# Folded products for the mixers' output gates and branch gates

## What is computed

```python
h = rmsnorm_2(x, mix_norm[l])
hq, hf, hi, hg, aq, ak, av, ga, gb = jnp.split(h @ w_in[l], split_idx, axis=-1)
...
o_a = hgrn2_chunk_scan(q_a, k_a, v_a, log_f)
o_a = rms(o_a.reshape(b, t, HG_HEADS, HG_DV)).reshape(b, t, HG_WV)
o_a = o_a * hgrn_out_norm[l].astype(f32) * jax.nn.silu(hg.astype(f32))
y_a = o_a.astype(x.dtype) @ w_branch_a[l]
...
y_b = o_b.astype(x.dtype) @ w_branch_b[l]        # o_b: dilated window attention, 4 heads of 3 groups
merged = jax.nn.sigmoid(ga) * y_a + jax.nn.sigmoid(gb) * y_b
x = x + merged @ w_out[l]
```

## Time and profile before

| | |
|---|---|
| median of 3 runs | 3286.3 us (3283.62 to 3288.35) |
| the profiled execution's own time | 3285.39 us |
| its span in the profile | 3283.6 us |
| mean granted TensorE clock | 0.998 of full speed |
| PE busy | 3246.1 us, 99% |
| DVE busy | 2387.8 us, 73% |
| ACT busy | 1341.4 us, 41% |

### The profile page before, as it was taken

One profiled execution on the slowest core, in us unless ns is written; L12 is line 12 of the kernel. 1 busy time (PEld: TensorE's weight loads), 2 busy tenths in 40 slices (PEclk: granted clock), 3 DMA queues, 4 the chain that ended last, 5 costly groups with the idle time before them and its releaser, 6 DMA issues.

```text
span 3283.6 us, 49474 instructions
## 1 busy us (share of the span) xinstructions
PE 3246.1 (99%) x18769; PEld 2836.5 (86%) x18769; DVE 2387.8 (73%) x3047; ACT 1341.4 (41%) x1809; POOL 611.4 (19%) x514
## 2 busy tenths in 40 slices
PE   8999999999999999999999999999999999999999
PEld 4888888888888888888888899999888889999988
DVE  4877857868787635556778877866888886875887
ACT  3222233212232224333536455356645445446643
POOL 2212322202321130002223220000223230000122
PEclk9999999999999999999999999999999999999999
DMA  6645514645265433334665664435666665443664
GB/s 227 204 153 172 160 46 135 201 140 186 89 199 172 135 99 94 90 103 145 198 177 167 195 182 146 123 117 146 184 191 178 195 183 161 122 122 110 195 196 147
DMA packets 863528, 507.66 MB, mean 155 GB/s; under 512 B 15093, under 2 KB 843569, under 8 KB 863345
## 3 DMA queue, kind: packets, MB, share of 16 engines
q1 hardware_dynamic: 862976, 503.74, 51.5%
q0 software_dynamic: 368, 1.38, 0.1%
HBM read 504.01 MB, written 1.05 MB: 154 GB/s over the span
## 4 chain that ended last, share of the span: by engine, by line
PE 92%; DVE 4%; ACT 2%; issue 1%; SPq 0%; DMA 0%; DVEq 0%; ACTq 0%
PE bank L661 18%; PE bank L663 18%; PE bank L662 18%; PE bank L659 17%; PE bank L657 10%; PE bank L656 2%; PE bank L1112 2%; DVE wlo_all L1508 1%; PE bank L776 1%; PE bank L966 1%; ACT whi_all L1179 1%; DVE t_full L1682 1%; PE bank L1005 1%; PE bank L1010 0%; PE bank L907 0%
## 5 line engine op out<-in xcount | busy, mean ns | idle before, releaser
L1508 DVE TENSOR_TENSOR wlo_all<-raw,whi_all 128x1024 fp32r<-128x1024 f32 (+3 forms) x768 | 1007.0, 1313 | 493.2 <-ACT whi_all L1179 490.7
L1179 ACT CAST whi_all<-raw 128x1024 fp32r<-128x1024 f32 (+3 forms) x768 | 834.4, 1090 | 896.6 <-PE bank L663 563.8
L661 PE MATMUL bank<-xn_two,whi_all 128*128 128x512 f32 (+1 forms) x2592 | 894.0, 345 | 2.9 <-DVE xn_two L1674 2.6
L663 PE MATMUL bank<-xn_two,wlo_all 128*128 128x512 f32 (+1 forms) x2592 | 872.5, 337 | 0.0
L662 PE MATMUL bank<-xn_two,whi_all 128*128 128x512 f32 (+1 forms) x2592 | 872.5, 337 | 0.0
L659 PE MATMUL bank<-xn_two,whi_all 128*128 128x512 f32 x1540 | 549.3, 396 | 0.0
L661 PEld LDWEIGHTS bank<-xn_two,whi_all 128*128 128x128 f32 x2592 | 491.4, 190 | 55.3 <-issue 4.3
L662 PEld LDWEIGHTS bank<-xn_two,whi_all 128*128 128x128 f32 x2592 | 491.5, 190 | 51.0 <-issue 0.7
L663 PEld LDWEIGHTS bank<-xn_two,wlo_all 128*128 128x128 f32 x2592 | 490.9, 189 | 51.5
L657 PE MATMUL bank<-xn_two,wlo_all 128*128 128x256 f32 x1760 | 455.7, 279 | 1.0 <-DVE xn_two L1674 0.9
L2148 POOL CAST h_two<-silu_g 128x256 f32 (+1 forms) x176 | 202.7, 1152 | 1339.8 <-DVE silu_g L1740 771.6
(11 more groups left out here) (323 smaller groups left out, 4280.1 us busy)
## 6 DMA issues: line engine op xcount, KB each, us to landing
raw<-in_ffn_w_in SPq DMA_DIRECT2D x176, 512.0 KB, 3.7
raw<-in_w_in SPq DMA_DIRECT2D x168, 512.0 KB, 3.7
ada_w<-in_ada_w SPq DMA_DIRECT2D x128, 512.0 KB, 3.7
raw<-in_ffn_w_gate SPq DMA_DIRECT2D x88, 512.0 KB, 3.7
raw<-in_ffn_w_up SPq DMA_DIRECT2D x88, 512.0 KB, 3.8
raw<-in_ffn_w_down SPq DMA_DIRECT2D x32, 768.0 KB, 5.1
raw<-in_ret_w_in SPq DMA_DIRECT2D x48, 512.0 KB, 3.9
raw<-in_ffn_w_out SPq DMA_DIRECT2D x32, 768.0 KB, 5.2
```

The lines of the kernel that those rows point to most:

```text
L661: pe.matmul(o, whi[s][:, k, :], hi, start=(k == 0), stop=False)
L663: return pe.matmul(o, wlo[s][:, k, :], hi, start=False, stop=(k == ks - 1))
L1179: act.copy(whi[s][:, 0:ks, :], raw[s][:, 0:ks, :]).then_inc(hi_done[s], 1)
L1508: tt(wlo[s][:, 0:ks, :], raw[s][:, 0:ks, :], whi[s][:, 0:ks, :].bitcast(F32), ALU.subtract).then_inc(lo_done[s], 1)
```

## The change

The units of `hg` and `gates` use folded products. DVE adds the bank's halves with one `tensor_reduce` into the gate's own tile and frees the bank; ACT does `split_hi` first, waits for that sum, and applies Silu or Sigmoid in place. A counter `gf` tells DVE how many gates are done. Besides, the semaphore `onehot_ready` is gone, and PE's first `sum` of a mixer waits for `zero`, which POOL raises a little later in its own order.

```diff
                 gained, ready = normed(a["norm"])
                 moving = pair(xn2_two, SEQ)
+                beside = pair(xn2_two, SEQ, True)
...
-                    source = dict(br_b=attended, hf=gained).get(ph, moving)
+                    source = dict(br_b=attended, hf=gained, hg=beside, gates=beside).get(ph, moving)
...
                     if c == 0:
-                        pe.wait_ge(onehot_ready, 1)
+                        pe.wait_ge(hg["zero"], l + 1)
...
-                def take(dst, func):
-                    def evacuate(s, k, r):
-                        act.activation(dst[:, k, :], bank[s][:, 0:SEQ], func).then_inc(bank_free[s], 1)
-                    return evacuate
+                def take_output_gate(s, k, r):
+                    act.wait_ge(bank_free[s], r + 2)
+                    act.activation(g_g[:, k, :], g_g[:, k, :], ACT.Silu).then_inc(hg["gf"], 1)
...
                 def take_gates(s, k, r):
                     dst = gates_a[:, k, :] if k < DC else gates_b[:, k - DC, :]
-                    act.activation(dst, bank[s][:, 0:SEQ], ACT.Sigmoid).then_inc(bank_free[s], 1)
+                    act.wait_ge(bank_free[s], r + 2)
+                    act.activation(dst, dst, ACT.Sigmoid).then_inc(hg["gf"], 1)
...
-                    if ph in ("hq", "hf"):
+                    if ph in ("hq", "hf", "hg", "gates"):
                         split_hi(s, r + 1, p["ks"] if it + 1 < p["rounds"] else next_ks[p["name"]])
                         takes[ph](s, SLOTS * it + s, r)
                         return
...
+                def gated(n):
+
+                    dve.wait_ge(hg["gf"], 3 * HH * l + n)
...
+                    if ph in ("hg", "gates"):
+                        dst = g_g[:, k, :] if ph == "hg" else gates_a[:, k, :] if k < DC else gates_b[:, k - DC, :]
+                        dve.tensor_reduce(dst, bank[s][:].rearrange("p (c t) -> p t c", c=2), AXX,
+                                          ALU.add).then_inc(bank_free[s], 1)
                     if ph == "br_b":
-                        after_act("gates", 2 + it, s)
+                        gated(2 * HH + k + 1)
...
                     if j == 0:
-                        for s in range(SLOTS):
-                            after_act("hg", 1, s)
+                        gated(HH)
...
                     link(pool.memset(onehot, 0.0))
                     link.after()
-                    pool.memset(onehot[:, P - 1:P], 1.0).then_inc(onehot_ready, 1)
+                    link(pool.memset(onehot[:, P - 1:P], 1.0))
+                    link.after()
```

More of the change, by code:

```diff
@@ L470, in build @@
         hg = {k: sem(f"hg_{k}") for k in ("d", "mm", "cp", "x", "xe", "o", "oe", "sq", "ss", "rt", "rr", "sp",
-                                          "hm", "of", "ohi", "olo", "mf", "mhi", "mlo", "zero", "qf")}
-        onehot_ready = sem("onehot_ready")
+                                          "hm", "of", "ohi", "olo", "mf", "mhi", "mlo", "zero", "qf", "gf")}
         lb_d = sem("lb_d")
@@ L1392, in do_mixer @@
                 takes = dict(att_qk=take_qk, hi=take_values(0), att_v=take_values(2), hq=take_query,
-                             hf=take_forget, hg=take(g_g, ACT.Silu), gates=take_gates)
+                             hf=take_forget, hg=take_output_gate, gates=take_gates)
                 def apply(k):
```

## The result

The changed kernel takes 3291.82 us (median of 20 runs, 3289.54 to 3294.07); the kernel before, run beside it, takes 3286.01 us (median of 20, 3283.51 to 3288.91). The ratio is 1.0017 with a 95% interval of 1.0011 to 1.0023: 5.8 us slower, clearly not nothing, and a little under the 6.6 us that the prediction set as its own bound for "slower".

A forecast was written before the change was run, and what follows sets the result against it. PE's own work plus its waits was taken to bound the kernel. Per mixer, 5.2 us more waiting less 1.7 gained gives 3.5, both 7.0: 3285.4 becomes 3292.4, or 3293 on the runs' median; range 3286 to 3299.

The forecast's parts named there:

- the walk: Likeliest case (chance 0.52): following the engines' lists, six points per mixer where PE waits come later; 3292.4 us.
- PE's gain: Folded units on PE save 0.07 us each: 1.7 us a mixer, 3.4 us in all.
- Step 1: hsum: split_hi and an open table load at unit 60 delay ACT's copies 1.4 us; PE waits 0.3 us.
- Step 2: hspread(3): unit 63's sum and gate precede round 0's exponentials; PE's shift 0.74 us, 0.9 more waiting.
- Step 3: turn_probs of round 1: ACT from unit 68 to scale takes 8.9 us, was 7.31; PE waits 1.8 us more.
- Steps 4 and 6: attend, rounds 1 and 2: ACT waits for DVE's sums of units 71 and 76; PE waits 0.8 and 1.1 more.
- Step 5: turn_probs of round 2: no load laid open, only order; shift 3.0 us, PE waits 0.4 us more.
- The end of the mixer: After attend of round 2, seven units at -0.07 us follow; the mixer ends 3.5 us later.
- Costs taken at nothing: PE's wait on zero, DVE's gated waits and PE's waits for a bank were each charged 0 us.
- Half of it: Rival (chance 0.28): a load stays hidden or sums slip into gaps; 1.3 to 2 us a mixer less, 3289.
- DVE falls behind: Rival (chance 0.07): late split_lo makes PE wait for weights, 4.9 us a mixer, 3302 us.
- A switch that stands open costs twice as much: Rival (chance 0.05): each newly opened table load holds ACT 2.7 us, not 1.29; 3298 us.

The follow-up runs named there:

- experiment 8: Experiment 6 with plain products and DVE's copy in place of the sum of halves, so without folding: 3278.69 us, ratio 0.9977.
- experiment 6: Changed kernel with ACT's in-place gate functions put off and run as one group a round, behind side work: 3276.05 us, ratio 0.9967.
- experiment 3: Changed kernel plus a one-column function ahead of ACT's wait for units 60 and 68, loading the tables early: 3289.14 us, ratio 1.0011.
- experiment 9: Changed kernel with only unit 63's gate function moved behind round 0's exponentials: 3290.25 us, ratio 1.0012.
- experiment 10: Kernel before, with only split_hi put ahead of the function in hg and gates; no folding, no DVE work: 3288.42 us, ratio 1.0007.
- experiment 7: Experiment 3 with only the gate functions of units 71 and 76 put behind their unit's side work: 3284.75 us, ratio 0.9996.

## Why the prediction was right, and where it was off

The forecast was 3293 us (7.0 us slower); it is 3291.8 (5.8 slower, 6.1 in the stretch). The likeliest case, the walk, is what happened. Its mechanism was shown step by step, not only its sum.

*PE's gain.* Taken as 0.07 us a unit, it is 0.075 (experiment 8): 0.08 in a row of units, as the earlier trace rows against the earlier trace rows had given, and about 0.06 for one that begins behind side work (2.90 us against 2.96 for unit 67 in experiments 6 and 8). So this term was right, and it explains nothing of the difference between 7.0 and 6.1. That lies in steps 2 to 6: each was 0.1 to 0.2 us too large, 0.7 us in a mixer, and at the end of the mixer 0.2 us less came back than I had said, which by luck made the sum look better than its steps.

*Step 1, hsum:* +0.28 for +0.2, and gone when the load is hidden (experiment 3).

*Step 2, hspread(3):* +0.54 for +0.74. Unit 63's gate is the cause of the rise there (experiment 9 takes +0.54 to -0.05). Experiment 3 brings this point to +0.06 with that gate in its place, but by another way: PE comes there 0.4 us earlier because hsum does, and the rise from hspread(2) to hspread(3) stays (+0.43, for +0.50 in the changed kernel and -0.11 in experiment 9). The exponentials' load came as late as forecast: 2192.03 against 2190.31, less the 0.87 us of the profile's own lateness, is 0.85 for 0.84. But from that load to the last split_hi ahead of hspread(3) it is 6.83 us (2198.86, shown in experiment 9) against 7.07 in the earlier trace rows: the gate of unit 65, now behind this split_hi, gave back 0.24 where I had counted 0.10.

*Step 3, turn_probs of round 1:* +1.34 over step 2 for the +1.5 of the walk. The chain took 8.81 us for 8.9, and unit 68 ended 0.4 us late for 0.6. A load laid open, shown twice: taken away from the changed kernel, 1.39 us (experiment 3), and added to the kernel before, +1.41 (experiment 10).

*Steps 4 and 6, the attends:* +0.58 and +0.89 for +0.7 and +1.0, from two gates queued ahead of the copies and waiting for DVE (experiment 7 takes both away). ACT in round 2, in answer to the earlier trace rows:

```profile
2248.72 0.42 ACT L1381 ACTIVATE gates_b<-gates_b 128x256 f32<-128x256 f32 x1 [0.71 <-DVE gates_b L1897]
2249.04 1.22 ACT L1442 COPY a_pt<-bank 128x512 f32<-128x512 f32 x3
```

Scale began at 2243.86, so it is 5.18 us to the copies: 5.3 in the walk, 4.28 before.

*Step 5, turn_probs of round 2:* the step that was wrong in kind, if only by a tenth. I charged order +0.1; it is -0.04. From the exponentials to scale it is 4.20 us after and 4.16 before: no load is laid open and the gate that moved behind split_hi costs nothing there.

*The end of the mixer:* it returned 0.27 us where I had said 0.5. I had counted seven changed units behind attend of round 2, and there are six (78 to 83), 0.45 us; why the rest didn't come back was not looked into. Two more slips changed nothing: the added waits of the walk sum to 5.3 us and not 5.2, and four of its six points, not three, are places where the earlier trace rows show a wait.

*Costs taken at nothing.* They were nothing: in both mixers PE has no new wait for a bank, for wlo_all or for `zero`. The sum of halves took 0.69 us as in the earlier trace rows.

*The rivals.* "Half of it" was wrong: no load slipped back by itself, it takes an instruction to pull it (experiment 3). "Folding gives nothing" fell with experiment 8. "DVE falls behind" had no sign in the waits. "A switch that stands open costs twice as much" asked for some 2.7 us at a load laid open, and experiment 10 has 1.41; of the drain that the Trainium skill gives in "ScalarE: Activation LUTs", What ACT_TABLE_LOAD costs, neither this run nor any other here shows anything. Had it held, the stretch would have been near +11.6.

*What I overlooked.* The prediction finds no wait of today that is shortened. For the change as it was made that is right. But the change also takes the bank's release away from ACT, and with it the reason for running the functions at once. That is worth 16 us between the changed kernel and experiment 6 (17 in the stretch), more than anything in the forecast.

## What to carry to other kernels

Fold products where the engine that multiplies does not wait; elsewhere a part of the saving (0.08 us in 2.88) is paid out in waiting, and the moved work decides. When a bank's emptying moves to another engine, the function that follows has lost its hurry: take it out of the strict list, and run several under one table load in time in which ACT waits anyway. And walk the list at the few places where PE waits: two gates of sixteen and two loads laid open made up most of the cost, and the busy shares (41% and 73%) showed none of it.

## What the runs showed of the hardware that I had not expected

- A table load whose function is the next in ACT's list runs ahead of that function's wait for another engine: at 2207.77 for a gate at 2212.22. With a cast between (unit 68 after: cast 2213.48, load 2214.55) it comes behind the cast's wait. A function of one column that waits for nothing pulls it ahead again (load at 2209.91, cast at 2214.27 in experiment 3). Laid open where PE waited for the chain, it cost 1.3 to 1.4 us.
- A stop of PE costs more than its recorded idle time. The earlier trace rows give 2.5 us a mixer; with all of it gone and the products unchanged (experiment 8) the first mixer is 3.5 us shorter. A matmul's record is 0.28 us long while the next starts 0.12 us after it, so a part of each stop lies under the last record's tail. At attend of round 2 of the kernel before the whole stop is hidden there:

```profile
2245.85 0.28 PE L663 MATMUL bank<-xn_two,wlo_all 128*128 128x256 f32 x1
2246.14 0.48 PE L1095 MATMUL bank<-a_pt,w_f 128*128 128x256 f32 x1
```

  Counted as the distance between two starts less 0.12 us, the five stops of the first mixer are 1.27, 0.37, 1.20, 0.36 and 0.17 us, 3.4 together. Experiment 8 is 3.8 us ahead at the end of the changed units, before its own wait for weights. Most of the remaining 0.4 us is in the groups right behind the stops, which take longer too (attend's first half 1.40 us from start to start in rounds 1 and 2, 1.30 in round 3, ahead of which PE doesn't stop).
- Folded, a step is a matmul of 512 columns and one of 256, together 0.35 us, against 0.36 for three of 256. Two folded units in a row, the first matmul of each:

```profile
2257.12 0.40 PE L655 MATMUL bank<-xn_two,whi_all 128*128 128x512 f32 x1
...
2259.91 0.39 PE L655 MATMUL bank<-xn_two,whi_all 128*128 128x512 f32 x1
```

2.79 us from start to start, 0.09 under the 2.88 of the earlier trace rows.
